# First norm of a two-block transformer layer: squares summed on VectorE, one total on TensorE

## The chip, the cores and the metric

The kernel runs on one core of a Trainium2 chip. The core has TensorE (matrix products into PSUM), VectorE, ScalarE and GpSimd for elementwise work, SyncE, which here only issues transfers, and 16 DMA engines. In the profile TensorE is PE (its weight loads PEld), VectorE DVE, ScalarE ACT, GpSimd POOL and SyncE SP. The metric is the device time of one execution in microseconds (us), lower being better.

## The reference

Two transformer blocks over 1024 tokens of 1024 features, in fp32: a block with pooling, sparse attention, memory attention and a gated feed-forward layer, and a block with two kinds of attention and a feed-forward layer. What matters here is the first operation of the first block and what reads it:

```python
def _rmsnorm(x, g):
    y = x * lax.rsqrt(jnp.mean(x * x, axis=-1, keepdims=True) + EPS)
    return y * g
...
h = _rmsnorm(x, norm_mix_pre)     # x: 1024 tokens x 1024 features
proj = h @ w_in
```

## The kernel before

Activations lie transposed: features on the 128 partitions, in KT = 8 tiles of 128 features, with the 1024 tokens along the free dimension. A mean over features is therefore a sum over partitions and over the eight tiles. TensorE makes it with a matrix of ones (`over_features`, L554: two fp32 matmuls of 512 columns, each shown as two passes in the profile), which leaves the sum in every partition of the PSUM region `wide(2)`.

The engines run programs of their own, written out by hand, and meet only at semaphores. There is no planner; the order in each program is the order of issue.

ScalarE first issues the four transfers of x (L1171, two tiles each, 1 MB) and eight small ones for constants (L1175). Then `squares` (L1142, instruction L1149) squares tile k into `tmp[k % 2]`. It waits for the transfer of that tile, and from tile 2 on for `n_added`, that is for TensorE's total of tile k-2, since there are two `tmp` buffers. On TensorE `total` calls `total_tile` for each of the eight tiles; each adds a tile's squares into the same PSUM region (L557). When the eighth is done, `inverse(0)` on ScalarE computes (total/1024 + eps)^-0.5 into `acc` in two instructions (Ln, L1160, and Exp, L1161). `acc` is a 128 x 1024 tile that is not in use before that.

After the totals TensorE makes two small products of bias tables (L583, L584), which wait for the constants and for a cast on VectorE (L1678). ScalarE copies them out (L1181, L1182) behind the Exp, issues two small stores, and goes on with `round_hi`.

VectorE's `scaled` multiplies each x tile by its gain and by `acc` (L1663). ScalarE rounds the result to the short fp32 format of TensorE (`h_hi`, L1168), and VectorE makes the rest (`h_lo`, L1657). Each fp32 product is then three matmuls (L519 to L521: hi by hi, lo by hi, hi by lo). `first_tiles` on TensorE uses normed tile k as soon as it is ready, for two weight slabs at once.

Weights come in slabs of 512 KB through two buffers `w_raw`, loaded by SP (L358, L363). GpSimd splits each slab into `w_hi` (L416) and `w_lo` (L419) with the same idea. The first two slabs are split as soon as they land; the third waits for the end of the first products on its buffer (`w_used`), and SP's load of a slab waits for the split of the slab that had the buffer before (`w_split`).

In the later norms after a sublayer, the squares are already added on VectorE (`add_square`, L1649: `acc` plus `tmp`), with one total at the end (`total_added`). Their instructions are of the same kind and shape as those of the change.

Of the kernel before, what the change touches and what calls it, by code (L numbers as in the profile page):

```python
# [20 lines left out]
ACT = mybir.ActivationFunctionType  # L21
ALU = mybir.AluOpType
# [4 lines left out]
KT = D // P  # L27
# [77 lines left out]
def program(nc, t):  # L105

    out = t["out"]
    with ExitStack() as ctx:
        def sem(name):
            return ctx.enter_context(nc.semaphore(name))  # L110
# [11 lines left out]
        def at(name, offset, shape, dt=F32):  # L122
            return nc.alloc_sbuf_tensor_at(name, shape, dt, offset=offset)

        def small(name, shape, dt=F32):
            size = int(np.prod(shape[1:])) * (2 if dt == BF16 else 4)
            here = place[0]
            place[0] += -(-size // 32) * 32
            return at(name, here, shape, dt)
# [6 lines left out]
        acc = small("acc", [P, S])  # L136
        tmp_at = place[0]
        tmp = [small(f"tmp{i}", [P, S]) for i in range(2)]
# [4 lines left out]
        ones = small("ones", [P, P])  # L143
# [20 lines left out]
        x_in = at("x_in", XR, [P, KT, S])  # L164
# [92 lines left out]
        def wide(slot):  # L257

            return ps[:, 2 * slot:2 * slot + 2, :].rearrange("p b n -> p (b n)")
# [30 lines left out]
        x_in_landed = [sem(f"x_in_landed{i}") for i in range(4)]  # L290
        dve_consts = sem("dve_consts")
        dve_step = sem("dve_step")
        n_sq, n_added = sem("norm_squared"), sem("norm_added")
        n_post_sq, n_acc = sem("norm_post_squared"), sem("norm_post_added")
        n_sum, n_rs = sem("norm_total"), sem("norm_inverse")
# [219 lines left out]
        def _(pe):  # L515
# [49 lines left out]
            def total_tile(name, k):  # L565

                tiles, before = PRE[name]
                pe.wait_ge(n_sq, before + k + 1)
                over_features(wide(2), tmp[k % 2], ones[:], k == 0, k == tiles - 1).then_inc(
                    n_sum if k == tiles - 1 else n_added, 1)  # L570

            def total(name):

                for k in range(PRE[name][0]):
                    total_tile(name, k)


            pe.wait_ge(dve_consts, 1)
            total("mix_pre")
            pe.wait_ge(consts_in, 16 * N_CONSTS)  # L580
            pe.wait_ge(dve_consts, 2)

# [555 lines left out]
        def _(act):  # L1138
# [3 lines left out]
            def squares(name, src, ready):  # L1142

                tiles, before = PRE[name]
                for k in range(tiles):
                    act.wait_ge(*ready(k))
                    if k >= 2:
                        act.wait_ge(n_added, before - PRE_ORDER.index(name) + k - 1)
                    nc.scalar.activation(tmp[k % 2][:], src(k), ACT.Square).then_inc(n_sq, 1)  # L1149
# [7 lines left out]
            def inverse(r, width=D):  # L1157

                act.wait_ge(n_sum, r + 1)
                step(nc.scalar.activation(acc[:], wide(2), ACT.Ln, bias=eps[:], scale=1.0 / width))  # L1160
                nc.scalar.activation(acc[:], acc[:], ACT.Exp, scale=-0.5).then_inc(n_rs, 1)  # L1161
# [13 lines left out]
                act.dma_start(dst[:], t[name]).then_inc(consts_in, 16)  # L1175

            act.wait_ge(dve_consts, 1)
            squares("mix_pre", lambda k: x_in[:, k, :], lambda k: (x_in_landed[k // 2], 16))
            inverse(0)
            act.wait_ge(frow_done, 1)  # L1180
            step(nc.scalar.activation(frow[:], ps[0:HEADS, 6, 0:384], ACT.Copy))  # L1181
# [458 lines left out]
        def _(dve):  # L1640
            step = Chain(dve, dve_step)
            tt, ts, stt = nc.vector.tensor_tensor, nc.vector.tensor_scalar, nc.vector.scalar_tensor_tensor
# [31 lines left out]

            nc.vector.memset(eps[:], EPS)
            nc.vector.memset(ones[:], 1.0).then_inc(dve_consts, 1)
            dve.wait_ge(consts_in, 16 * N_CONSTS)
            nc.vector.tensor_copy(ident16[:], ident[:]).then_inc(dve_consts, 1)  # L1678
            dve.wait_ge(dve_consts, 2)
# [606 lines left out]
```

## Time and profile before

| | |
|---|---|
| median of 3 runs | 3357.95 us (3356.92 to 3360.74) |
| span of the profiled execution, first to last instruction | 3358.0 us |
| mean granted TensorE clock | 0.974 |
| PE busy | 3155.6 us, 94% |
| DVE busy | 1537.2 us, 46% |
| ACT busy | 816.2 us, 24% |
| POOL busy | 1206.1 us, 36% |

The profile is of one execution, whose span agrees with the median of the timed runs. Times in its rows are counted from the start of the span. Busy shares are means over the whole kernel, and tell little of a stage of some 30 us at its start.

### The profile page before, as it was taken

What the parts mean: (1) busy time and instruction counts of PE and PEld (TensorE: products, weight loads), DVE (VectorE), ACT (ScalarE), POOL (GpSimd) and SP (SyncE); (2) the same over time, 40 slices, a digit from 0 to 9 for tenths busy, and PEclk for the clock granted to TensorE, in tenths of its full rate; (3) what the DMA queues carried; (4) which work ended last, traced back from release to release, by engine and by line L of the source; (5) the groups of instructions that cost most, each with busy time, mean ns of one, the idle gap of its engine ahead of it and who ended that gap; (6) DMA issues with size and microseconds to landing.
All of it is one profiled execution on the core that took longest, in us unless ns stands there. A gap on an engine that the chain in (4) does not pass through costs nothing.

```text
span 3358.0 us, 34815 instructions
## 1 busy us (share of the span) xinstructions
PE 3155.6 (94%) x13555; PEld 2467.7 (73%) x13566; DVE 1537.2 (46%) x2220; ACT 816.2 (24%) x1186; POOL 1206.1 (36%) x567
## 2 busy tenths in 40 slices
PE   7999998999878799999999799889998999999999
PEld 5787775678656588888887477568666788888887
DVE  3799956553643621221122621255884532232236
ACT  3312215511224301000001332245774100000000
POOL 2254342334722244344333133173002344444443
PEclk9899999999989999999999899999999999999999
DMA  2022310034110011111111122442421111111111
GB/s 103 26 88 100 139 44 7 1 138 150 63 38 19 25 49 46 50 50 44 50 50 44 40 75 100 123 150 69 106 76 72 44 45 50 50 50 44 50 50 75
DMA packets 69272, 217.54 MB, mean 65 GB/s; under 512 B 7468, under 2 KB 18900, under 8 KB 68408
## 3 DMA queue, kind: packets, MB, share of 16 engines
q1 hardware_dynamic: 40832, 145.51, 14.0%
q10 hardware_dynamic: 28344, 70.74, 5.7%
q8 instruction: 62, 1.02, 0.1%
q14 instruction: 34, 0.28, 0.0%
HBM read 175.31 MB, written 40.65 MB: 64 GB/s over the span
## 4 chain that ended last, share of the span: by engine, by line
PE 87%; DVE 6%; ACT 4%; issue 1%; POOL 1%; ACTq 0%; DMA 0%; POOLq 0%; DVEq 0%
PE ps L519 25%; PE ps L521 25%; PE ps L520 25%; PE ps L557 3%; PE ps L720 2%; DVE y L1672 1%; PE ps L1036 1%; PE ps L1024 1%; DVE x L1673 1%; PE ps L710 1%; PE ps L1009 1%; POOL w_lo L419 1%; PE ps L1010 1%; DVE acc L1649 0%; POOL w_hi L416 0%
## 5 line engine op out<-in xcount | busy, mean ns | idle before, releaser
L416 POOL TENSOR_TENSOR w_hi<-w_raw,zero 128x1024 fp32r<-128x1024 f32 x210 | 407.5, 1940 | 1808.9 <-PE ps L521 1801.9
L519 PE MATMUL ps<-normed_hi,w_hi 128*128 128x512 f32 x1488 | 588.8, 396 | 34.7 <-DVE normed_lo L1657 18.2
L520 PE MATMUL ps<-normed_lo,w_hi 128*128 128x512 f32 x1488 | 583.7, 392 | 0.0
L521 PE MATMUL ps<-normed_hi,w_lo 128*128 128x512 f32 x1488 | 583.6, 392 | 0.0
L419 POOL TENSOR_TENSOR w_lo<-w_raw,w_hi 128x1024 fp32r<-128x1024 f32 x210 | 564.4, 2687 | 16.5
L519 PEld LDWEIGHTS ps<-normed_hi,w_hi 128*128 128x128 f32 x1488 | 282.5, 190 | 100.3 <-issue 28.6
L519 PE MATMUL ps<-hidden_hi,w_hi 128*128 128x512 f32 x864 | 336.9, 390 | 2.8 <-DVE hidden_lo L1888 2.8
L521 PE MATMUL ps<-hidden_hi,w_lo 128*128 128x512 f32 x864 | 336.8, 390 | 0.0
L520 PE MATMUL ps<-hidden_lo,w_hi 128*128 128x512 f32 x864 | 336.6, 390 | 0.0
L520 PEld LDWEIGHTS ps<-normed_lo,w_hi 128*128 128x128 f32 x1488 | 282.5, 190 | 60.8 <-issue 2.2
L521 PEld LDWEIGHTS ps<-normed_hi,w_lo 128*128 128x128 f32 x1488 | 282.2, 190 | 59.4
L519 PE MATMUL ps<-h_hi,w_hi 128*128 128x512 f32 x528 | 208.7, 395 | 8.3 <-DVE h_lo L1657 5.0
L520 PE MATMUL ps<-h_lo,w_hi 128*128 128x512 f32 x528 | 207.5, 393 | 0.0
L521 PE MATMUL ps<-h_hi,w_lo 128*128 128x512 f32 x528 | 207.5, 393 | 0.0
L1886 DVE TENSOR_TENSOR tmp<-tmp,ps 128x1024 f32<-128x1024 f32 x22 | 26.9, 1222 | 369.1 <-PE ps L521 367.6
L519 PEld LDWEIGHTS ps<-hidden_hi,w_hi 128*128 128x128 f32 x864 | 162.6, 188 | 37.0 <-DVE hidden_lo L1888 3.2
L520 PEld LDWEIGHTS ps<-hidden_lo,w_hi 128*128 128x128 f32 x864 | 162.6, 188 | 33.7
L521 PEld LDWEIGHTS ps<-hidden_hi,w_lo 128*128 128x128 f32 x864 | 162.6, 188 | 33.8
L2100 DVE TENSOR_TENSOR y<-y,ps 128x1024 f32<-128x1024 f32 x64 | 78.1, 1221 | 206.6 <-PE ps L521 205.6
L1731 DVE MATCH_REPLACE8 score<-top,score 128x1024 f32<-128x1024 f32 (+2 forms) x192 | 166.8, 877 | 0.0
L2092 DVE TENSOR_TENSOR tmp<-tmp 128x1024 f32<-128x1024 f32 x32 | 60.3, 1883 | 220.4 <-ACT tmp L1631 220.4
L1727 DVE MAX8 top<-score 128x8 f32<-128x1024 f32 (+2 forms) x192 | 161.1, 882 | 0.0
(360 smaller groups left out, 5179.9 us busy)
## 6 DMA issues: line engine op xcount, KB each, us to landing
w_raw<-weights_dram SPq DMA_DIRECT2D x228, 512.0 KB, 3.7
gates_scratch<-tmp ACTq DMA_DIRECT2D x24, 512.0 KB, 2.7
gated<-gates_scratch ACTq DMA_DIRECT2D x24, 512.0 KB, 5.4
head_part<-diff_qk_scratch SPq DMA_DIRECT2D x48, 256.0 KB, 6.4
x_in<-x_dram ACTq DMA_DIRECT2D x4, 1024.0 KB, 11.1
x<-x_dram ACTq DMA_DIRECT2D x1, 4096.0 KB, 13.9
diff_qk_scratch<-d_hi ACTq DMA_DIRECT2D x8, 512.0 KB, 2.7
diff_qk_scratch<-d_out ACTq DMA_DIRECT2D x8, 512.0 KB, 2.7
```

The source lines that it names most:

```text
L416: nc.gpsimd.tensor_tensor(w_hi[s][:], raw[s][:], zero[:, 0:1].broadcast_to([P, 1024]), ALU.add).then_inc(w_rounded, 1)
L419: nc.gpsimd.tensor_tensor(w_lo[s][:], raw[s][:], w_hi[s][:].bitcast(F32), ALU.subtract).then_inc(w_split, 1)
L519: nc.tensor.matmul(out, sh, mh, start=start, stop=False)
L520: nc.tensor.matmul(out, sh, ml, start=False, stop=False)
L521: return nc.tensor.matmul(out, sl, mh, start=False, stop=stop)
L557: last = nc.tensor.matmul(out[:, n:n + HALF], lhs, src[:, n:n + HALF], start=start, stop=stop)
L710: last = nc.tensor.transpose(ps[:, 4 + n_tr % 2, q * P:(q + 1) * P], mix_rows[group % 2][q][:, j * P:(j + 1) * P], ident[:])
L720: nc.tensor.matmul(ps[:, 6 + group % 2, :], value[:, j, :], probs_t[n_tr % 2][:], start=j == 0, stop=j == group // 2).then_inc(pv_done, 1)
L1727: nc.vector.max(top8[:, e, :], sc).then_inc(dve_step, 1)
L1731: nc.vector.match_replace(sc, top8[:, e, :], sc, TAKEN).then_inc(dve_step, 1)
L2092: tt(part[:], part[:], part[:], ALU.mult).then_inc(u_sq, 1)
L2100: tt(y[:, m, :], y[:, m, :], wide(m % 4), ALU.add).then_inc(u_added, 1)
```

## The change

VectorE now sums the squares of the eight tiles. ScalarE squares tile 0 straight into `acc` and the others into the two `tmp` buffers; from tile 3 on it waits for the add that frees its buffer. VectorE adds tiles 1 to 7 into `acc`, each add after the square and after the add before it. TensorE makes one total from `acc` when the seventh add is done. `n_added` is raised seven times as before, now by VectorE. The adds stand in VectorE's program ahead of its wait for the constants and of the cast L1678. Nothing of the other norms changes.

```diff
@@ TensorE
             pe.wait_ge(dve_consts, 1)
-            total("mix_pre")
+            pe.wait_ge(n_added, KT - 1)
+            over_features(wide(2), acc, ones[:]).then_inc(n_sum, 1)
             pe.wait_ge(consts_in, 16 * N_CONSTS)
@@ ScalarE
             act.wait_ge(dve_consts, 1)
-            squares("mix_pre", lambda k: x_in[:, k, :], lambda k: (x_in_landed[k // 2], 16))
+            for k in range(KT):
+                act.wait_ge(x_in_landed[k // 2], 16)
+                if k >= 3:
+                    act.wait_ge(n_added, k - 2)
+                nc.scalar.activation(tmp[k % 2][:] if k else acc[:], x_in[:, k, :], ACT.Square).then_inc(n_sq, 1)
             inverse(0)
@@ VectorE
             nc.vector.memset(ones[:], 1.0).then_inc(dve_consts, 1)
+            for k in range(1, KT):
+                dve.wait_ge(n_sq, k + 1)
+                if k >= 2:
+                    dve.wait_ge(n_added, k - 1)
+                tt(acc[:], acc[:], tmp[k % 2][:], ALU.add).then_inc(n_added, 1)
             dve.wait_ge(consts_in, 16 * N_CONSTS)
```

## Rows read from the trace of the kernel before

**Rows 1.** The page: busy time of each engine, and the chain's shares.

```profile
PE 3155.6 (94%) x13555; PEld 2467.7 (73%) x13566; DVE 1537.2 (46%) x2220; ACT 816.2 (24%) x1186; POOL 1206.1 (36%) x567
...
PE 87%; DVE 6%; ACT 4%; issue 1%; POOL 1%; ACTq 0%; DMA 0%; POOLq 0%; DVEq 0%
```

**Rows 2.** Chain that ended last, first 60 us: start, length (us), what.

```profile
7.82 1.06 ACT tmp L1149
9.02 15.56 PE ps L557 x32
24.61 1.12 ACT acc L1160
...
29.78 1.24 DVE h_lo L1657
...
32.34 0.43 PE ps L521
...
40.10 0.23 PE ps L520
...
54.36 1.87 POOL w_hi L416
```

**Rows 3.** Timeline of ScalarE, 7 to 29 us: start, length, instruction, idle before.

```profile
14.37 1.06 ACT L1149 ACTIVATE tmp<-x_in 128x1024 f32<-128x1024 f32 x1 [0.66 <-PE ps L557]
...
26.71 0.46 ACT L1181 ACTIVATE frow<-ps 8x384 f32<-8x384 f32 x1
```

**Rows 4.** Tile x_in: transfers issued up to 1.7 us, then the last (2.2).

```profile
L1171 ACTq DMA_DIRECT2D x_in<-x_dram x3: 403/445/453, 0.8 to 1.7; - x3
...
DMA to landing us min/median/max: 7.0/10.1/12.1
...
DMA to landing us min/median/max: 14.5/14.5/14.5
```

**Rows 5.** Chain that ended last, 1850 to 1900 us, adds of a later norm.

```profile
1854.16 1.21 DVE acc L1649
...
1856.43 1.86 DVE acc L1649
```

**Rows 6.** Timeline of VectorE, 1858.3 to 1866 us.

```profile
1858.38 3.17 DVE L1649 TENSOR_TENSOR acc<-acc,tmp 128x1024 f32<-128x1024 f32 x1
```

**Rows 7.** Timeline of GpSimd, 1843 to 1862 us.

```profile
1857.27 3.20 POOL L419 TENSOR_TENSOR w_lo<-w_raw,w_hi 128x1024 fp32r<-128x1024 f32 x1
```

**Rows 8.** Line L416, whole span: durations in ns, min/median/max.

```profile
L416 POOL TENSOR_TENSOR w_hi<-w_raw,zero x210: 1892/1895/2879, 7.4 to 3329.4; 128x1024 fp32r<-128x1024 f32 x105
```

**Rows 9.** Timeline of GpSimd, first 100 us: the first two slabs.

```profile
9.36 2.35 POOL L419 TENSOR_TENSOR w_lo<-w_raw,w_hi 128x1024 fp32r<-128x1024 f32 x1
11.66 1.89 POOL L416 TENSOR_TENSOR w_hi<-w_raw,zero 128x1024 fp32r<-128x1024 f32 x1
13.64 2.37 POOL L419 TENSOR_TENSOR w_lo<-w_raw,w_hi 128x1024 fp32r<-128x1024 f32 x1
```

**Rows 10.** Timeline of TensorE, 1859 to 1893 us: two totals of later norms.

```profile
1861.61 3.78 PE L557 MATMUL ps<-acc,ones 128*128 128x512 f32 x4 [6.39 <-DVE acc L1649]
...
1888.54 1.98 PE L557 MATMUL ps<-tmp,ones 128*128 128x512 f32 x4 [0.47 <-ACT tmp L1149]
```

**Rows 11.** Timeline of TensorE, first 32 us: the small table products.

```profile
25.15 1.02 PE L584 MATMUL ps<-onehot,table 32*4 32x512 f32 x2
```

**Rows 12.** Timeline of VectorE, first 75 us.

```profile
20.38 0.23 DVE L1678 CAST ident<-ident 128x128 bf16<-128x128 f32 x1 [19.34 <-DMA onehot<-c_onehot_dram]
```

**Rows 13.** Windows: engines' busy time, granted clock (PEclk), DMA share, GB/s.

```profile
core 0: us, PE busy (x) PEld busy (x) DVE busy (x) ACT busy (x) POOL busy (x), PEclk, DMA share, GB/s
26.20:31.15 4.95, 0.00 (x0) 0.03 (x1) 3.81 (x4) 3.57 (x5) 0.00 (x0) 0.81 0.02 4
31.15:37.00 5.85, 5.85 (x16) 4.60 (x17) 5.78 (x5) 2.11 (x2) 0.00 (x0) 0.58 0.00 0
58.80:65.00 6.20, 6.20 (x20) 4.99 (x21) 2.74 (x2) 0.44 (x1) 4.94 (x2) 0.72 0.28 89
...
1896.50:1902.00 5.50, 5.43 (x17) 4.42 (x18) 5.43 (x5) 2.12 (x2) 0.00 (x0) 0.70 0.00 0
```

## The prediction

> **What bounds the kernel now.** I read the page first: TensorE is busy 94% of the span and holds 87% of the chain that ended last, VectorE 6%, ScalarE 4% [rows 1]. So only what delays or advances TensorE's next work counts. The change sits in the first 28 us, where TensorE is not yet streaming products, so I then read the chain of that stretch alone [rows 2]. It runs: the first x transfer lands and ScalarE squares tile 0 (7.82), TensorE makes totals from 9.02 to 24.58 (32 passes, four to a tile), ScalarE turns the total into the inverse root (24.61, two instructions), VectorE and ScalarE make the first normed tile, and the first product starts after the VectorE instruction of 29.78. The next link after those products is the weight split at 54.36, which waits for TensorE and not for a clock time of its own. I take from this that whatever moves the ScalarE instruction at 24.61 moves everything behind it by as much: the normed tiles, the first products, the split at 54.36, and all later stages, which wait on each other.
>
> What paces 9.02 to 24.58? In ScalarE's timeline [rows 3] a square starts each 1.72 us and had waited 0.66 us for TensorE: TensorE's total of a tile is the pace, not the squares (1.06 us). The transfers are not: the first of the four (two tiles each) lands 7.0 us after its issue at 0.78, the second 10.1 after about 1.2 (11.3), the third 12.1 after 1.7 (13.8), the last 14.5 after 2.2 (16.7) [rows 4]. The square of tile 3 stands at 14.37, so at that pace tile 6's comes at 19.5, long after the last transfer.
>
> **The change, part by part.** It removes seven of the eight totals from TensorE. It adds seven adds to VectorE, each waiting for a square and for the add before it, and a new order: one total starts when the last add is done. Square k from 3 on now waits for add k-2, square 2 for nothing but its data.
>
> *An add alone.* The same instruction, same shape, stands in the later norms: 1.21 us with GpSimd idle [rows 5]. From the end of one add to the start of a dependent one I take 0.10 us: two adds from 1856.43 follow on each other, the second starts at 1858.38 [rows 6] and the first, 1.86 long in the chain, ends at 1858.28. So 1.31 us a step when nothing else hinders.
>
> *An add beside a GpSimd split.* This is the term that decides. The add of 1858.38 took 3.17 us, to 1861.55 [rows 6]. GpSimd's w_lo instruction began at 1857.27 and took 3.20 [rows 7], where with VectorE idle it takes 2.37 [rows 9]; w_hi's longest of 210 is 2.88 against 1.89 [rows 8]. The sizes fit one picture: the two instructions never run together. The add of 1856.43 ended at 1858.28; w_lo, waiting, then ran to 1860.47; the waiting add then ran 1.08 to 1861.55. So an add that waits behind GpSimd ends 1.08 us after GpSimd's instruction, and GpSimd's next then ends 2.19 (w_lo) after the add or, since w_lo got by with 0.18 less than 2.37, 1.71 (w_hi). In the first 16 us GpSimd splits the first two slabs: w_lo from 9.36, w_hi from 11.66, w_lo from 13.64 for 2.37 [rows 9], exactly where the first adds fall. Step by step:
> add 1: squares 0 and 1 are done at 9.82; w_lo holds to 11.71; ends 12.79.
> w_hi: 12.79 + 1.71 = 14.50. Add 2 (square 2 is done at 12.4, from 11.3 plus 1.06): ends 15.58.
> w_lo: 15.58 + 2.19 = 17.77. Add 3: ends 18.85. GpSimd then has nothing till the first products are done.
> adds 4 to 7: 18.85 + 4 x 1.31 = 24.09. The squares keep up: square 7 starts when add 5 is done (21.47) and ends at 22.6, before add 7's start at 22.9.
> So the sum of squares is complete at 24.1, almost when all eight totals were done before.
>
> The Trainium skill, GPSIMD Engine Reference, section Specifications, says that GpSimd shares its SBUF interfaces with VectorE and contends with instructions that have two SBUF inputs, but gives no price. VectorE: DVE Perf Modes, the section on the TRN2 errata, gives (N+151)/0.96 ns for an fp32 add: 1.22 us here, which the 1.21 row agrees with. By that figure alone the adds would be done where the next paragraph's lower bound has them.
>
> *The lower bound of this term.* With every add at 1.21 plus 0.10: add 1 from 9.87, square 2 from 11.3, square 4 from 13.8, square 6 behind the last transfer at 16.7, add 6 from 17.9, add 7 to 20.4. The upper bound is the 24.1 plus a few tenths of waits, 24.4. I take 24.1, since the nearest rows are the same instruction against the same two GpSimd instructions.
>
> *The one total.* TensorE has done nothing before it, and after idling the nearest row is 3.78 us for the four passes of such a total after an idle 6.4 us, against 1.98 of the same after a wait of 0.5 [rows 10]. Start 24.09 + 0.06, then 3.78, and 0.04 to ScalarE: 27.97 in place of 24.61. That is +3.4 us (lower bound: 20.4 + 3.9 = 24.3, or -0.3).
>
> The Trainium skill, TensorE: Matmul & The Clock Gate, Part 1 (the clock gate), says that the throttled state is the default and that activity releases it. It speaks against this change: what remains on TensorE is a short burst from idle. With the total at 1.98 the sum would come out 1.8 us lower; the row of 3.78 after idling agrees with the page.
>
> *The two small table products.* They follow the total on TensorE, and ScalarE needs them 2.1 us after 24.61 (its frow copy starts at 26.71, [rows 3]). Before, they ran from about 24.5, the last of them from 25.15 for 1.02 [rows 11]: done by 26.17, 0.5 us early. At 1.2 GHz they double to about 3.0 us, 31.0 in place of a need at 30.1: +0.9. If the clock rises on the way, 0. Elsewhere the low level lasted 3.3 to 4.9 us after a gap (below, [rows 13]), which falls near 27.5 to 29 here: I take +0.1. The cast that these products also wait for now stands behind the adds on VectorE (before: 20.38, behind the last small transfer [rows 12]); it comes at about 24.2 and takes 0.23, hidden under the total.
>
> *GpSimd and its queue, SP.* The splits end 1.8 us later (17.8 for 16.0), and SP issues the loads of the next two slabs up to 1.8 us later, as each waits for a split. The first products start no earlier than 31, the next slabs are split after 54: both hidden by over 10 us. Nothing else moves.
>
> *The clock behind it.* TensorE idles from about 30 to 34.5, and before from 26.2 to 31.15; the granted clock fell in that gap (0.81 over it) and the first products ran low: 0.58 over 5.85 us is 4.9 us at the lower level. Other starts after a gap: 0.72 over 6.2 (3.5 us) and 0.70 over 5.5 (3.3) [rows 13]. The mean of the three is 3.9. A product takes 0.43 us of the chain low and 0.23 high [rows 2], so a low microsecond costs 0.47. The stretch of before is the longest of the three; a mean one saves (4.9 - 3.9) x 0.47 = 0.5. Bounds: none low, -2.3; half again as long, +1.2.
>
> **Sum.** +3.4 + 0.1 - 0.5 = +3.0 us. The profiled span is 3358.0, the median of the runs shown is 3357.95, so they can stand for each other: **3361 us**.
>
> **Rivals.**
> 1. *The adds run freely beside GpSimd.* For: the ordinary add is 1.21, and many lie beside other instructions. Against: both adds of [rows 5, 6] beside a split are stretched. Then -0.3, tables +0.1 to +0.9 (the constants land at about 20.3, late enough to matter little), clock -0.5: 3357.5.
> 2. *TensorE stays at 2.4 GHz through the gap* after the late burst, since that gap is somewhat shorter (4.4 for 4.95). Then +3.5 - 2.3 = +1.2: 3359. Against: it fell in the gap before.
> 3. *Slower by over 0.2%: the clock stays low in the first products.* One late total and two small products may leave TensorE low for longer. The stage has 96 products (8 tiles, 2 slabs, 2 halves, 3 each), some 85 of them at 0.23 before; all at 0.43 would add 85 x 0.20 = 17 us: 3378. It decides from 3364.7: (6.7 - 3.5) / 0.47 = 6.8 low microseconds more than the 4.9. Against: none of the three stretches of [rows 13] passes 5 us.
> 4. *A clear gain.* If the totals were 15.5 us of pure pacing and seven of eight were saved, 13 us would go. It can't: the last x lands at 16.7, two squares (the second 1.06 later), an add and a total even of 1.98 give 22.1, at most 2.5 us before 24.61; with the clock's 2.3 that is 4.8. So no mechanism that I see reaches 0.2%.
>
> **How the numbers follow.** A measurement of this kernel tells about 0.2% (6.7 us) from no change; its three runs already spread over 3.8 us. Forecast (splits and adds take turns, low total): 0.64. Rival 1: 0.17. Rival 2: 0.08. Rival 3: 0.07. Something else, either way: 0.04. The range goes from rival 1 less a microsecond of spread (3356.5) to the forecast's upper ends (+3.7 + 0.9 + 1.2 = 5.8 and a microsecond of spread): 3365. Faster by over 0.2%: 0.02; slower: 0.09 (rival 3 and the top of the forecast); within: 0.89.
>
> **What the profile after would show.** The first add ends near 12.8 and the first three take 2 to 3 us, the last four 1.21; w_hi from 11.66 and w_lo behind it are stretched to about 2.9 and 3.3. The only total starts near 24.2, takes 3.8 us, and ScalarE's Ln instruction stands near 28.0. The first product starts near 34.5 in place of 31.15, and the distance from there to later stages is that of before but for the low stretch. Wrong would be: adds of 1.2 beside the splits (Ln near 24.3), a squares wait that paces the adds, a total of 2 us, or ScalarE waiting over 0.5 us for the table products.

## The result, and the profile after

| | before | changed |
|---|---|---|
| median | 3357.97 us (21 runs) | 3363.16 us (21 runs) |
| ratio of the two, 95% interval | | 1.0018 (1.0011 to 1.0024) |
| span of the profiled execution | 3358.0 us | 3362.6 us |
| mean granted clock | 0.974 | 0.973 |

The change makes the kernel 5.2 us slower by the medians. That is inside the range of 3356.5 to 3365, and just within the 0.2% that I had called no change, but its interval lies wholly above 1. The profiled execution itself took 3364.4 us: a span is 1.8 us shorter than the device time of the same execution. So the profile of before, with a span of 3358.0, is of an execution near 3359.8, 2 us slower than its median; that it equals the median of 3358.0 is a coincidence, and the two can't stand for each other as the prediction has it.

The chain that ended last, changed kernel, first 62 us (start, length, what), beside [rows 2]:

```profile
7.64 1.06 ACT acc L1183
8.70 0.95 ACT tmp L1183
9.67 2.95 DVE acc L1686
12.72 2.73 DVE acc L1686
15.54 3.20 DVE acc L1686
18.84 1.24 DVE acc L1686
20.16 1.24 DVE acc L1686
...
22.82 1.23 DVE acc L1686
24.20 3.76 PE ps L557 x4
27.98 1.12 ACT acc L1161
...
33.16 1.24 DVE h_lo L1662
34.54 0.77 PE ps L519
...
57.57 1.87 POOL w_hi L416
```

The whole chain of this stretch has moved from TensorE to VectorE. Three adds take 2.7 to 3.2 us, four take 1.24, and the one total takes 3.76. The Ln instruction stands at 27.98 in place of 24.61, the first product at 34.54, and the split behind the first products at 57.57 in place of 54.36 [rows 2].

GpSimd's timeline of the changed kernel, beside [rows 9]:

```profile
9.19 2.34 POOL L419 TENSOR_TENSOR w_lo<-w_raw,w_hi 128x1024 fp32r<-128x1024 f32 x1
11.48 2.87 POOL L416 TENSOR_TENSOR w_hi<-w_raw,zero 128x1024 fp32r<-128x1024 f32 x1
14.44 3.21 POOL L419 TENSOR_TENSOR w_lo<-w_raw,w_hi 128x1024 fp32r<-128x1024 f32 x1
```

The first w_lo is as before, since add 1 waits for it (9.67 to 12.62). The next two are stretched by 0.98 and 0.84: each begins while an add is still running, and the next add waits in turn.

TensorE's timeline of the changed kernel, beside [rows 10, 11], and windows over the total and over its first products, beside [rows 13]:

```profile
24.20 3.75 PE L557 MATMUL ps<-acc,ones 128*128 128x512 f32 x4 [24.20 <-DVE ident L1688]
27.88 1.28 PE L584 MATMUL ps<-onehot,table 32*8 32x384 f32 x2
29.00 1.02 PE L585 MATMUL ps<-onehot,table 32*4 32x512 f32 x2
```

```profile
24.20:27.95 3.75, 3.75 (x5) 1.21 (x6) 0.00 (x0) 0.00 (x0) 0.00 (x0) 1.00 0.00 0
34.54:40.00 5.46, 5.46 (x15) 4.32 (x16) 5.39 (x5) 2.12 (x2) 0.00 (x0) 0.58 0.00 0
```

The releaser named for the total is the cast at 23.97; in the code the total waits only for the seventh add, which ended at 24.05, so it was that add. The small products were done at 30.02, just in time for ScalarE at 30.09. The first products ran at the lower level for 4.6 us (0.58 over 5.46), 0.3 us less than before.

One thing these rows don't agree on is the clock of the total: its granted clock is given as 1.00, though its four passes take 3.75 us, as long as those of [rows 10], over which the granted clock was 0.50 (1861.61 to 1865.40, kernel before). In these profiles the granted clock reads 1.00 in every window ahead of about 24 us, also where passes take double, and in e2_late_slab it does so still over the first products (32 to 37 us). So in this stretch, until the granted clock first falls, "the lower level" is read here from the length of the passes, not from the granted clock.

So up to 57 us the profile is the forecast. What is open is the rest: the profiles differ by 4.6 us and the medians by 5.2, where the first norm accounts for 3.2. The experiments went after both: which part makes the 3.4 us, and whether anything further on belongs to the change.

### The profile page after: what moved, and what is told of

The parts are those of the page before. It is cut to its first block, busy times and chain, and to the rows that moved or that the text cites. A ratio compares the mean times of both kernels' runs of the same rounds, so it can differ in the third digit from the quotient of the medians.

```text
span 3362.6 us, 34782 instructions
## 1 busy us (share of the span) xinstructions
PE 3145.5 (94%) x13538; PEld 2463.3 (73%) x13538; DVE 1548.9 (46%) x2227; ACT 816.2 (24%) x1186; POOL 1207.2 (36%) x567
## 4 chain that ended last, share of the span: by engine, by line
PE 86%; DVE 7%; ACT 4%; issue 1%; POOL 1%; ACTq 0%; DMA 0%; POOLq 0%; DVEq 0%
PE ps L519 25%; PE ps L521 25%; PE ps L520 25%; PE ps L557 2%; PE ps L721 2%; DVE y L1677 1%; PE ps L1037 1%; PE ps L1025 1%; DVE x L1678 1%; PE ps L711 1%; PE ps L1010 1%; POOL w_lo L419 1%; PE ps L1011 1%; DVE acc L1654 0%; POOL w_hi L416 0%
## 5 line engine op out<-in xcount | busy, mean ns | idle before, releaser
L416 POOL TENSOR_TENSOR w_hi<-w_raw,zero 128x1024 fp32r<-128x1024 f32 x210 | 408.0, 1943 | 1810.3 <-PE ps L521 1803.6
```

What stands on the lines that cost most here:

```text
L416: nc.gpsimd.tensor_tensor(w_hi[s][:], raw[s][:], zero[:, 0:1].broadcast_to([P, 1024]), ALU.add).then_inc(w_rounded, 1)
```

## The experiments

Ratios are to the kernel before, timed beside it on the same chip. Each kernel was timed in 11 or 12 runs, the kernel before in 33 or 35.

### e1_pure_delay and e10_delay_again: only later

```diff
+            act.wait_ge(n_sum, 1)
+            for _ in range(3):
+                step(nc.scalar.activation(tmp[0][:], x_in[:, 0, :], ACT.Square))
             inverse(0)
```

The three squares are extra work on the kernel before; nothing else is changed.

> The kernel before, with three extra squares (1.06 us each, chained) on ScalarE between the total and its Ln instruction: a pure delay of 3.2 to 3.4 us at the place where the change is late by 3.4. Theory 'pure shift' (all of the change's cost is the lateness of that instruction, and everything behind it keeps its distance): Ln near 27.9, and the run is slower than before by 3.3 us, 0.10%, give or take 1 us, and level with the changed kernel. Rival 'more than the shift' (the changed order costs something further downstream, since its measured ratio of 1.0018 is 6 us): the delay alone costs 3.3 us and the run stays 2 to 3 us faster than the changed kernel.

> The pure delay of three squares before Ln, once more, for a smaller error. Theory 'pure shift': together with the first measurement 3.3 to 4.5 us over before, and no less than the changed kernel by more than a microsecond. Rival 'more than the shift': 3.3 over before, while the changed kernel stands at 6.

Measured: 1.0019 (1.0010 to 1.0028), and 1.0014 (1.0005 to 1.0023). The 22 runs have a mean of 3361.7 us. All runs of the kernel before in this study, 133 with those of e5_before_again, have a mean of 3357.6, so the delay costs 4.2 us, with a standard error of 0.7. The edit adds 3 x 1.09 = 3.3, and in the two profiles the split behind the first products comes 4.7 and 4.1 us later, as the eight totals also took longer (16.59 and 16.13 for 15.56). That fits a pure shift. The first ratio is as high as the changed kernel's, the second lower; neither tells the theories apart alone.

The surprise is in the two profiles. Chain of e10_delay_again, its last totals and delay:

```profile
8.97 16.13 PE ps L557 x32
25.12 1.06 ACT tmp L1181
...
28.39 1.12 ACT acc L1160
...
58.45 1.87 POOL w_hi L416
```

Here the split comes 4.1 us after that of [rows 2], and yet both profiled executions were among the fastest of their kernel (spans 3356.5 and 3355.7). Most of the lead comes from one place, the stage that ranks the keys. Its row in windows of the kernel before, and under it the same stretch of e10_delay_again, 4 us later:

```profile
90.00:120.00 30.00, 28.73 (x99) 22.27 (x98) 20.15 (x28) 14.44 (x21) 0.00 (x0) 0.51 0.02 7
```

```profile
94.00:124.00 30.00, 29.34 (x119) 22.16 (x118) 18.71 (x27) 13.52 (x20) 0.00 (x0) 0.77 0.00 1
```

GpSimd's timeline of the same two kernels, the splits in front of and behind that stage:

```profile
83.39 1.90 POOL L416 TENSOR_TENSOR w_hi<-w_raw,zero 128x1024 fp32r<-128x1024 f32 x1 [7.28 <-PE ps L521]
131.09 1.90 POOL L416 TENSOR_TENSOR w_hi<-w_raw,zero 128x1024 fp32r<-128x1024 f32 x1 [43.35 <-PE ps L521]
```

```profile
85.86 1.90 POOL L416 TENSOR_TENSOR w_hi<-w_raw,zero 128x1024 fp32r<-128x1024 f32 x1 [7.28 <-PE ps L521]
128.47 1.90 POOL L416 TENSOR_TENSOR w_hi<-w_raw,zero 128x1024 fp32r<-128x1024 f32 x1 [38.26 <-PE ps L521]
```

From one to the other it is 47.7 us in the first and 42.6 in the second, over the same instructions: a clock of 0.51 or 0.77 in this stage goes with 5.1 us, more than the change costs in its own place. Another 1.6 us were won ahead of it, between the splits at 58.61 and 71.73 of the kernel before (granted clock from 60 to 90 us: 0.94, and 1.00 in e10_delay_again). A difference of spans between two single profiles therefore proves nothing here; the places must be compared one by one, and the end to end by many runs.

### e2_late_slab and e12_late_slab_again: the adds without GpSimd

```diff
             for s in range(2):
                 pool.wait_ge(raw_landed[s], 16)
+                if s == 1:
+                    pool.wait_ge(n_added, KT - 1)
                 split(s, s + 1)
```

> The changed kernel, with GpSimd's split of the second slab held back until the seventh add is done. Theory 'taking turns' (an add and a split never run together): only the first add still waits, for the first slab's w_lo, and ends near 12.6; adds 2 to 7 take 1.21 us each, the last is done near 20.5 in place of 24.05, the Ln instruction stands near 24.4, and the run is 3.6 us (0.11%) faster than the changed kernel, level with before. Rival 'the squares and the transfers pace the adds': the last add comes no earlier than 23, and under 1 us is won. Price of the edit: the second slab's split then ends near 25, before its first use at 31.

> The changed kernel with the second slab's split held back, once more. Its Ln instruction stands at the time of before (24.51 against 24.61), yet it measured 1.0012. Theory 'pure shift': that was scatter, and the second measurement falls to 1.0000 to 1.0007. Rival 'more than the shift': 1.0008 or more again, so that a kernel with the change's code is slower than before even when the first norm is as early.

Measured: 1.0012 (1.0002 to 1.0021), and 1.0006 (0.9997 to 1.0015). Chain of e2_late_slab:

```profile
9.65 2.96 DVE acc L1688
12.71 1.23 DVE acc L1688
...
19.35 1.23 DVE acc L1688
20.72 3.75 PE ps L559 x4
24.48 1.37 PE ps L586 x2
25.85 1.72 PE ps L587 x2
```

With GpSimd out of the way only the first add waits, and the last is done at 20.58, 3.5 us sooner, as the theory of taking turns has it. Squares and transfers don't pace the adds. The 22 runs have a mean of 3360.7 against 3363.9 for the 33 of the changed kernel: 3.2 us won (standard error 0.7), where 3.5 less the next point, 2.5, was to be had.

The next point is the term that I had bounded with 0 and 0.9. Here the small products are as long as at the lower level throughout (1.37 and 1.72) and end at 27.57, where ScalarE was ready for them about 26.6. The first product stands at 32.05, 0.9 us behind that of before, though Ln is 0.1 ahead of it. So this kernel should cost 0.9 over before; its 22 runs lie 3.1 over (0.6). The second measurement alone, 1.0006, is inside what the pure shift allowed; the two together are not.

### e3_warm_total: TensorE busy before the total

```diff
...
+            for added, n in ((2, 2), (3, 1), (4, 1), (5, 1), (6, 1)):
+                pe.wait_ge(n_added, added)
+                keep_busy(n)
             pe.wait_ge(n_added, KT - 1)
```

`keep_busy(n)`, whose definition is left out here, makes n matmuls of `ones` by 512 columns of x into `wide(0)`. Its products are extra and never read.

> The changed kernel, with six more matmuls of 512 fp32 columns on TensorE (ones times x, into a PSUM region that is overwritten later), spread over the waits for adds 2 to 6. Theory 'cold burst': the total then runs at the higher level and takes 2.0 us in place of 3.75, Ln near 26.2 in place of 27.98, and the run is 1.8 us faster than the changed kernel. Rival 'a lone total costs 3.75 us whatever TensorE did before': Ln stays near 28.0 and the time as it is.

Measured: 1.0008 (0.9999 to 1.0017). TensorE's timeline:

```profile
22.59 1.12 PE L581 MATMUL ps<-x_in,ones 128*128 128x512 f32 x2 [0.20 <-DVE acc L1693]
23.92 1.98 PE L557 MATMUL ps<-acc,ones 128*128 128x512 f32 x4 [0.20 <-DVE acc L1693]
25.84 0.81 PE L591 MATMUL ps<-onehot,table 32*8 32x384 f32 x2
```

The same total on the same operand takes 1.98 in place of 3.75, and Ln stands at 25.95: 2.0 us sooner. The mean of the 11 runs is 4.0 us below the changed kernel's (standard error 1.0), where 1.8 was expected. The rival, that a lone total costs 3.75 in any case, is out. The Trainium skill, TensorE: Matmul & The Clock Gate, Part 1, names the throttled state as the default; these two rows agree. They agree by the length of the passes alone, since the granted clock reads 1.00 over both totals.

### e4_warm_gap: TensorE busy before the first product

```diff
+            pe.wait_ge(n_rs, 1)
+            keep_busy(4)
             first_tiles("mix_in", "mix_pre", h1)
```

> The changed kernel, with four more matmuls of 512 fp32 columns on TensorE (3.4 us at the higher level) in the gap between the small table products and the first product, from the moment the inverse root is ready. Theory 'the gap costs the clock': the first products start at the same 34.5 but at 0.23 us each, the granted clock from 34.5 to 40 is 1.0 in place of 0.57, the third slab's split starts 2.1 us sooner (55.4 in place of 57.55), and the run is 2.1 us faster than the changed kernel. Rival: the fill itself runs at the lower level (6.9 us) and pushes the first product to 37.

Measured: 1.0013 (1.0004 to 1.0022); the mean is 1.7 us below the changed kernel's (standard error 1.0), not clearly better. TensorE's timeline:

```profile
30.96 6.44 PE L589 MATMUL ps<-x_in,ones 128*128 128x512 f32 x8
36.84 0.80 PE L519 MATMUL ps<-h_hi,w_hi 128*128 128x512 f32 x1
37.47 0.40 PE L520 MATMUL ps<-h_lo,w_hi 128*128 128x512 f32 x1
```

The rival came true, and the theory missed: the fill took 6.4 us, mostly in passes of the lower level's length, and held the first product to 36.84, 2.3 us behind that of the changed kernel. From there on every product is at the higher level. The split behind the first products came at 58.00 for 57.55 in GpSimd's timelines, so the products won 1.9 of the 2.3 us back and 0.4 were lost.

This profile shows one more thing. Up to the total it is the changed kernel, but its small table products ended at 31.03 (1.37 and 1.71 in the chain), and ScalarE waited 0.88 us for them.

### e5_before_again and e6_after_again: the two kernels once more

Both are unchanged copies, so there is no edit to show.

> The kernel before once more, unchanged, for a second profile and for the size of a difference that is none. So far every kernel whose first product starts at about the time of before, or later, measured 1 to 3 us slower than its start says. Theory 'pure shift, and the rest is scatter': the ratio to before is 1.000 within 0.0009, and the second profile of the same program differs from the first by a microsecond or two in places where its code is the same (the length of the low clock in the first totals and products, the hand-over of the last rope tile near 2210 us). Rival 'the change costs 2 us more downstream': the second profile repeats the first within 0.5 us everywhere, and the hand-over near 2210 takes 4.5 us again.

> The changed kernel once more, unchanged, beside the others of this call. Theory 'pure shift, and the rest is scatter': 1.0010 to 1.0018 of before; in its profile the adds, the total and the Ln instruction stand within 0.3 us of the first profile (Ln 27.98), while the distance from there to 2572 us differs by a microsecond or two from the first, since the hand-over near 2210 and the low stretches fall as they like. Rival 'more than the shift': 1.0018 or more, and the hand-over near 2210 is again the 5.4 us of the first profile or longer.

Measured: 0.9993 (0.9984 to 1.0002) for the same program against itself, and 1.0019 (1.0011 to 1.0028). The second profile of before stays within 0.3 us of the first up to 2131 us, and is 1.1 us later at the split of 2306. The chain of e6_after_again repeats the first profile to within 0.1 us up to the total:

```profile
22.86 1.22 DVE acc L1686
24.23 3.50 PE ps L557 x4
27.76 1.12 ACT acc L1161
...
56.70 1.87 POOL w_hi L416
```

The split comes at 56.70 here and 57.57 there, by the clock of the total and of the first products: +2.3 and +3.2 over before.

### e9_unused_adds: the change's VectorE work without its lateness

```diff
+            dve.wait_ge(x_in_landed[0], 16)
+            for k in range(1, KT):
+                step(tt(y[:, 0, :], x_in[:, 0, :], x_in[:, 1, :], ALU.add))
             dve.wait_ge(consts_in, 16 * N_CONSTS)
```

> The kernel before, totals on TensorE as they were, plus seven adds of two x tiles on VectorE at its idle start, chained, into a region that is overwritten later; their result is not used. It has the change's extra VectorE instructions and their collision with GpSimd's splits, but no later Ln. Theory 'pure shift': the adds take turns with the splits and end by 19 us, Ln stays near 24.6, and the run is level with before, 1.0000 within 0.0009. Rival 'more than the shift' (something in VectorE's longer program or the stretched splits costs 2 to 3 us further on): 1.0006 to 1.0010.

Measured: 1.0003 (0.9993 to 1.0013), no difference. The adds take turns with the splits as in the changed kernel (GpSimd's next three instructions take 3.20, 2.87 and 3.23), and cost nothing, as nothing waits for them. Ln stands at 25.71 and not at 24.6, since the totals ran low for longer (16.85 us in place of 15.56, with the same instructions); the split is at 54.48, as before.

### e7_late_slab_warm and e8_before_warm: both kernels with fills

e7 is e2, e3's fill at adds 1, 5 and 6 (4, 1 and 1 matmuls), and e4's fill. e8 is the kernel before with e4's fill and this:

```diff
             pe.wait_ge(dve_consts, 1)
+            for _ in range(24):
+                nc.tensor.matmul(wide(0)[:, 0:P], ones[:], ones[:], start=True, stop=True)
             total("mix_pre")
```

> The changed kernel with the second slab's split held back, with six filling matmuls before the total and four in the gap before the first product. Theory: the last add is done at 20.5, the total takes 2.0 (Ln near 22.6 in place of 27.98), the small products run at the higher level and are in time, the fill in the gap is done in 3.4 us before the first product is ready, and the first products run at 0.23 us each: the third slab's split starts near 50 in place of 57.55, and the run is 7 us faster than the changed kernel, 3 to 4 faster than before (0.9990). Rival: the fills run low and push the total or the first product, and under 3 us is won on the changed kernel.

> The kernel before (eight totals on TensorE), with 24 matmuls of 128 fp32 columns on TensorE while the first x transfer is under way, and four of 512 in the gap before the first product. Theory: the first total then takes 1.7 in place of 3.4 us, and from there one total starts each 1.72: Ln near 22.9 in place of 24.61; the first products start at the higher level and save 2.3: the third slab's split near 50.3 in place of 54.33, and the run is 3 to 4 us faster than before (0.9989), so that the totals on TensorE are no worse than adds on VectorE with everything done for the adds. Rival: TensorE drops to the lower level in the gap all the same, and 1.7 us is all that is won.

Measured: 0.9992 (0.9983 to 1.0000), and 0.9986 (0.9977 to 0.9995). TensorE's timeline of e8_before_warm:

```profile
1.10 6.99 PE L580 MATMUL ps<-ones 128*128 128x128 f32 x48 [1.10 <-DVE ones L1684]
8.87 14.10 PE L557 MATMUL ps<-tmp,ones 128*128 128x512 f32 x32 [0.78 <-ACT tmp L1157]
...
25.26 3.70 PE L590 MATMUL ps<-x_in,ones 128*128 128x512 f32 x8 [0.69 <-ACT acc L1169]
29.55 0.47 PE L519 MATMUL ps<-h_hi,w_hi 128*128 128x512 f32 x1 [0.59 <-DVE h_lo L1665]
```

Both do what the theory says in their place: Ln at 22.68 and 23.00 (e7, e8), the gap's fill in 3.70 us now that it starts at the higher level, the first product not held back, and the split near 50. e8, with its eight totals, is 4.3 us faster than before in the mean, and is the fastest kernel of this study together with the next. e7, 4.2 us ahead at that split, is only 2.4 faster in the mean (standard error 1.0).

### e11_pairs_warm: four pairs

Each square goes to a place of its own, VectorE adds tiles 2j and 2j+1, TensorE makes four totals, and fills stand before, between and behind them. The second slab's split waits for the last add. Of the edit, only TensorE's part is shown, without its end:

```diff
+            for _ in range(44):
+                nc.tensor.matmul(wide(0)[:, 0:P], ones[:], ones[:], start=True, stop=True)
+            for j in range(KT // 2):
+                pe.wait_ge(n_added, j + 1)
+                last = over_features(wide(2), y[:, 2 * j, :], ones[:], j == 0, j == KT // 2 - 1)
+                if j < KT // 2 - 1:
+                    keep_busy(1)
...
```

> A middle way: ScalarE squares each tile into a place of its own, VectorE adds them in four pairs that don't wait for each other, TensorE makes four totals; the second slab's split waits for the last add, and filling matmuls keep TensorE at the higher level before, between and after the totals. Theory: the last x transfer (16.5) now sets the end: square 7 at 18.7, the last add 20.0, the last total 22.0, Ln near 22.0 in place of 24.61 and 27.98; the third slab's split near 49.3; 5 us faster than before (0.9985). Rival: a fill or total at the lower level pushes Ln to 23 or later, and it is no better than the kernel before with fills (4 us).

Measured: 0.9988 (0.9979 to 0.9997). Its chain:

```profile
1.10 12.53 PE ps L586 x88
13.63 1.72 PE ps L559 x4
...
21.36 1.73 PE ps L559 x4
23.12 1.12 ACT acc L1176
```

The rival came true: the first fill lasted to 13.6, a microsecond longer than the first pair needed, and the three between the totals cost 0.86 each, so TensorE was never idle and Ln came at 23.1 and not 22.0. It is level with e8.

## Why the prediction was right, point by point

**An add alone**, 1.31 us a step: the last four steps run from 18.84 over 20.16 to 22.82: 1.33. Right.

**Adds and splits take turns.** The ends were worked out as 12.79, 15.58, 18.85 and 24.09; they are 12.62, 15.45, 18.74 and 24.05. The first is early because the first slab landed 0.17 sooner. Shown by e2_late_slab, which takes the collision away and gets the 3.5 us back; e9_unused_adds shows the same stretch of the splits without any cost. Rival 1, free adds, is out.

**The one total**, 3.78 from idle: 3.75, and 3.50 in the second profile. That its price comes from TensorE's idling before it is shown by e3_warm_total (1.98).

**The Ln instruction** was due at 27.97 and stands at 27.98 and 27.76: +3.4 and +3.2 us.

**The small products**, +0.1 of 0 to 0.9: nothing in either profile of the changed kernel (in the first with 0.07 us to spare), 0.9 to 1.0 in e4_warm_gap, whose order is the same up to there, and as much in e2_late_slab and e12_late_slab_again. The bounds were right to 0.1 us; within them the value differs from one execution to the next, so that +0.1 fitted was partly luck.

**GpSimd's queue and SP**: the splits ended at 17.65, forecast 17.8; the split of the third slab waited for the first products, as said, and not for this.

**The clock behind**, -0.5: from Ln to the split the changed kernel's two profiles won 0.2 and 0.8. Right in the mean. Rival 2, TensorE stays high through the gap, did not happen by itself; it takes a fill (e7, e8). Rival 3, a longer low stretch in the first products, did not happen: 4.6 us.

**The sum**, +3.0, is the step that is mis-sized. The local part came out at +3.2 and +2.3, but the median moved by 5.2. The 33 runs of the changed kernel lie 6.4 us over the 133 of before (standard error 0.6), a pure delay of 3.3 lies 4.2 over (0.7). My step "whatever moves the ScalarE instruction at 24.61 moves everything behind it by as much" holds for the order of work, but not for the time. By GpSimd's splits the changed kernel's two profiles were 3.2 and 2.3 us late at 54 us of the kernel before, 1.5 and 0.1 at 424, and 4.6 and 1.5 at 2672.

About 2 of the 6.4 us go with the clock. Each execution has a mean granted clock on record (for before, 112 of the 133). In 43 of those 112 it is 0.976 or more, with a mean time of 3354.2 us; in the other 69 it is lower, with 3359.6. Of the changed kernel's 33 executions only 2 reach 0.976, and of the 22 of e2_late_slab and e12_late_slab_again none. Among the executions below 0.976 the changed kernel is 4.4 us slower than before (standard error 0.5), the pure delay 3.4 (0.7), and the late slab 1.1 (0.5). The last two are near what each loses in its first norm; the changed kernel stays 1 to 2 us above its own 2.3 and 3.2. This sorts results and is no experiment: why a kernel gets the higher clock less often is not shown.

Another part may have a place. Near 2210 us ScalarE stores the last rope tile to memory, and attention starts when it has landed, which is on the chain that ended last. From the start of the store's issue to ScalarE's first attention instruction, in ScalarE's timeline of the kernel before and of the changed one:

```profile
2211.18 0.47 ACTq L1495 DMA_DIRECT2D mla_rope_scratch<-g_rope  x1
2217.02 1.11 ACT L1517 ACTIVATE rows<-ps,mstat 128x1024 f32<-128x1024 f32 x1 [9.48 <-DVE mstat L1973]
```

```profile
2214.60 1.49 ACTq L1500 DMA_DIRECT2D mla_rope_scratch<-g_rope  x1
2221.35 1.11 ACT L1522 ACTIVATE rows<-ps,mstat 128x1024 f32<-128x1024 f32 x1 [10.63 <-DVE mstat L1983]
```

That is 5.84 and 6.75 us. Over the profiles it is 5.55 to 6.46 in the six kernels whose VectorE does not sum the squares (before, e1, e5, e8, e9, e10), and 6.68 to 7.97 in the eight whose VectorE does (the changed kernel, e2 to e4, e6, e7, e11, e12). The two groups do not overlap; their means differ by 1.2 us. Over the wider stretch between GpSimd's splits on either side (2131 and 2306 us in the kernel before) they do overlap: against the first profile of before the six lie -0.8 to +0.9 us, the eight +0.3 to +3.5, the changed kernel at +2.8 and +0.3. So the row alone does not settle it. It is not the seven instructions on VectorE as such (e9 has them, at 5.85), and not a later start (e1 and e10). Why the same store, 2200 us behind the edit, takes longer in one group I cannot say, and no experiment of mine tells; it may be the layout of a program or chance. The three parts (2.3 to 3.2 in the first norm, 2 with the clock, about 1 here) make up the 6.4 us to within the error of the means, the last two without a shown cause.

## What to carry to other kernels

Before summing on VectorE to relieve TensorE, look at what paces the stretch and at what GpSimd does in it: seven adds of 1.2 us are no gain over seven totals of 1.7 when three of them must take turns with GpSimd's two-input instructions of 1.9 and 2.3 us. Even with two of the three collisions gone (e2_late_slab) Ln was only level with before. A lone product after idling costs twice its price (3.75 for 1.98 us), so "one in place of eight" saved less than it seemed, and a few products that nobody reads, placed so that they end in time and start at the higher level, made the kernel before 4.3 us faster, where the change made it slower (e8, 0.9986). Where a single stage can differ by 5.1 us between executions of the same instructions, compare places of two profiles and means of many runs, not spans.

## What the runs showed that I had not expected

That VectorE's adds and GpSimd's splits take turns was forecast; how regularly they do was not. In both profiles of the changed kernel, an add that waits ends 1.09 to 1.10 us after GpSimd's instruction, in each of the three collisions (2.95, 2.73 and 3.20 us for adds of 1.24). The Trainium skill, GPSIMD Engine Reference, Specifications, names the contention; the price is from these rows.

A fill of TensorE can lose as much as it wins. The same four matmuls in the same gap took 3.70 us when TensorE came to them from products at the higher level's length (e7, e8) and 6.44 when it came from a lone total after idling (e4).

The stage that ranks the keys ran at a granted clock of 0.77 in two of the 14 profiles (e1 and e10, 90 to 120 us) and of 0.50 to 0.58 in the other twelve, with the same instructions. The 5.1 us between the two are near the 5.5 that separate the executions of the kernel before with a mean granted clock of 0.976 or more from the others. That it is this stage there too is likely but not shown: both profiles of before are of executions at 0.974. A later arrival alone does not bring the higher clock: e1 and e10 come to the stage 3.2 and 2.5 us later than the kernel before, but the changed kernel comes 3.2 later too, at 0.56.
